# Gate and up as seven products of quadrant sums, and eight tile buffers for the first norm of a two-layer hybrid decoder kernel

## The reference

```python
    mix = jnp.concatenate([hm, ha, hs], axis=-1) @ w_out
    x = x + rms_norm(mix, norm_w[1])
    h = rms_norm(x, norm_w[2])
    ff = (jax.nn.silu(h @ w_gate) * (h @ w_up)) @ w_down
    return x + rms_norm(ff, norm_w[3])
```

## Time and profile before

| | us |
|---|---|
| median of 3 runs | 2903.09 |
| lowest and highest of the 3 | 2901.5 and 7317.59 |
| profiled execution, its own time | 2905.06 |
| profiled execution, span of the trace | 2903.3 |

### The profile page before, as it was taken

How to read it: one execution, slowest core, us unless ns; L and a number is a source line. 1 busy time by engine, 2 the same in 40 slices (tenths; PEclk the granted TensorE clock), 3 DMA queues, 4 the chain that set the end, 5 groups by cost and what they waited for, 6 DMA issues and landing times. The chain is left out here.

```text
span 2903.3 us, 34251 instructions
## 1 busy us (share of the span) xinstructions
PE 2810.1 (97%) x13396; PEld 2261.9 (78%) x13396; DVE 1229.7 (42%) x2170; ACT 924.5 (32%) x1618; POOL 906.3 (31%) x450
## 2 busy tenths in 40 slices
PE   6999999999999999999989999998999999999997
PEld 5677877778888888888766788777788888888886
DVE  4479854574111122211355799547640122211115
ACT  4336433563211111111243374346632111111112
POOL 1238410330332333222343383104303232222234
PEclk9999999899999999999999999999999999999999
DMA  4102310522211111111321133106221111111113
GB/s 131 44 23 87 116 57 19 151 88 95 74 44 51 58 43 58 43 43 43 116 80 30 30 95 111 59 15 179 81 89 50 58 44 57 43 43 43 51 45 137
DMA packets 232832, 197.72 MB, mean 68 GB/s; under 512 B 20352, under 2 KB 208896, under 8 KB 232592
## 3 DMA queue, kind: packets, MB, share of 16 engines
q1 hardware_dynamic: 226960, 175.26, 20.0%
q10 hardware_dynamic: 5760, 20.97, 1.9%
HBM read 157.41 MB, written 38.80 MB: 68 GB/s over the span
## 5 line engine op out<-in xcount | busy, mean ns | idle before, releaser
L2125 PE MATMUL ps<-act_hi,whi 128*128 128x512 f32 x1408 | 548.4, 389 | 0.0
L2125 PE MATMUL ps<-act_hi,wlo 128*128 128x512 f32 x1408 | 548.1, 389 | 0.0
L2125 PE MATMUL ps<-act_lo,whi 128*128 128x512 f32 x1408 | 547.7, 389 | 0.0
L2189 DVE TENSOR_TENSOR hf<-sg,ps 128x1024 f32<-128x1024 f32 x44 | 53.7, 1221 | 891.4 <-PE ps L2125 891.4
L834 PE MATMUL ps<-act_hi,whi 128*128 128x512 f32 x960 | 395.2, 412 | 15.5 <-ACT smr L383 10.6
L834 PE MATMUL ps<-act_hi,wlo 128*128 128x512 f32 x960 | 378.9, 395 | 0.0
L834 PE MATMUL ps<-act_lo,whi 128*128 128x512 f32 x960 | 378.6, 394 | 0.0
L2002 POOL TENSOR_TENSOR wlo<-raw,whi 128x1024 fp32r<-128x1024 f32 x88 | 210.0, 2395 | 489.3 <-ACT whi L2048 489.3
L1247 DVE TENSOR_SCALAR_CACHE_REDUCE ties<-score,kth 128x384 uint8<-128x384 f32 (+5 forms) x396 | 348.4, 943 | 5.1 <-issue 0.4
L2196 DVE TENSOR_TENSOR yacc<-yacc,ps 128x1024 f32<-128x1024 f32 x176 | 214.8, 1220 | 248.5 <-PE ps L2157 248.5
L2125 PEld LDWEIGHTS ps<-act_lo,whi 128*128 128x128 f32 x1408 | 264.3, 188 | 55.2
(11 more groups left out here) (304 smaller groups left out, 3974.6 us busy)
## 6 DMA issues: line engine op xcount, KB each, us to landing
raw<-in_w_in SPq DMA_DIRECT2D x56, 512.0 KB, 3.9
raw<-in_w_up SPq DMA_DIRECT2D x44, 512.0 KB, 4.0
raw<-in_w_gate SPq DMA_DIRECT2D x44, 512.0 KB, 3.8
raw<-in_w_down SPq DMA_DIRECT2D x44, 512.0 KB, 3.6
proj_scratch<-stage ACTq DMA_DIRECT2D x40, 512.0 KB, 2.7
wc<-proj_scratch SPq DMA_DIRECT2D x14, 1280.0 KB, 6.7
xmid_scratch<-xres SPq DMA_DIRECT2D x16, 512.0 KB, 2.6
resid<-xmid_scratch SPq DMA_DIRECT2D x14, 512.0 KB, 5.5
```

What stands on the lines that cost most here:

```text
L2125: mm = pe.matmul(ps[:, 2 * s + half, :], w[:, k], a[:, k, cols], start=(k == 0 and m == 0), stop=(k == KT - 1 and m == 2))
L2189: v.tensor_tensor(hf[:, :], sg[:, :], unit_psum(1), ALU.mult).then_inc(hidden.sem, 1)
```

## The change

**Seven products.** For a block of 256 columns the product (256 columns × 1024 inputs) × (1024 inputs × 1024 tokens) is seen as 2×2 quadrants: input halves of 512, column units of 128, token halves of 512. Instead of eight quadrant products it computes seven products of sums of quadrants, and forms the four result quadrants by adding and subtracting them. A product is 4 k-slices × 3 = 12 matmuls of the same shape as before; gate and up of a block are 14 products. The down part keeps its 96 matmuls per block.

- The seven token forms (`form_hi`, `form_lo`, 128×2048 each) are built once per layer at the end of D, by ACT, DVE and POOL: ACT now copies the transposed tile to `normed_q` in float32 (`untransposed`), DVE adds quadrants (`token_sum`), ACT rounds (`token_hi`), DVE or POOL subtracts (`token_lo`). Parts that need only tiles 0 to 6 (EARLIER, 3/4) are done apart from those of tile 7 (LAST, 1/4).
- The weight forms are built for every block: 10 sums on DVE (`form_sum_part`, 128×512), 14 copies on ACT (`form_hi_part`), 14 subtractions on POOL (`form_lo_part`), in a ring of six slots shared with the down weights. Slot reuse waits for the product five places earlier.
- Results are gathered in SBUF (`gate_t`, `up_t`): per seven products ACT does 2 copies out of PSUM (`first_product`) and DVE 10 adds or copies of 128×512 (`drain`). Silu and the multiplication then work from SBUF in four pieces of 128×512.
- The order on PE is: gate of block 0; then for each k up(k), gate(k+1), down(k); at the end up(10) and down(10) with nothing between. `hhi`/`hlo` have one buffer now. Weight loads are 1 MB each.
- POOL clears `yacc` only after the last token form, since the buffers overlap.

**Eight tile buffers.** In layer 0 the tiles 4 to 7 of x go to the not yet used `score` buffer, and all eight loads stand ahead of the small weights.

**Placement.** All of SBUF is laid out anew by address. The constants `cst` are loaded again in layer 1, the small weights of layer 1 are loaded at the end of E instead of the start, and the residual and norm row loads for the end of E wait for products of up(10).

```diff
-                    sp.dma_start(tap[t % 4][:, :], x_in[t * P:(t + 1) * P, :]).then_inc(xa_in[t % 4].sem, 16)
+                    sp.dma_start(x_place(t), x_in[t * P:(t + 1) * P, :]).then_inc(xa_in[t].sem, 16)
...
+        WEIGHT_SUM = {1: ((0, 1), (1, 1), ALU.subtract), 2: ((0, 0), (1, 1), ALU.add), 3: ((1, 0), (0, 0), ALU.subtract),
+                      4: ((1, 0), (1, 1), ALU.add), 6: ((0, 0), (0, 1), ALU.add)}
+        PRODUCT_BANK = (0, 1, 2, 3, 0, 1, 2)
+        DRAINED = {1: 2, 2: 4, 3: 6, 4: 7, 5: 9, 6: 10}
...
+                def product(i, f, slot, r):
+                    pe.wait_ge(*f_lo(L, f + 1))
+                    later = not (isinstance(r, int) and r == 0)
+                    if i == 0 and later:
+                        pe.wait_ge(*m_drain(L, 10 * (r - 1) + DRAINED[4]))
...
+                    if i == 4:
+                        pe.wait_ge(*m_first(L, r + 1))
+                    if i == 5:
+                        pe.wait_ge(*m_drain(L, 10 * r + DRAINED[1]))
...
+                    wh, wl = flat_form(ring_hi[slot]), flat_form(ring_lo[slot])
+                    for k in range(4):
+                        for m, (w, a) in enumerate(((wh, form_hi[i]), (wh, form_lo[i]), (wl, form_hi[i]))):
+                            mm = pe.matmul(ps[:, PRODUCT_BANK[i], :], w[:, k], a[:, k], start=(k == 0 and m == 0), stop=(k == 3 and m == 2))
+                    mm.then_inc(f_done.sem, 1)
...
+                pe.wait_ge(*t_lo_p(L, 2))
                 pe.wait_ge(*d_mix(L, NT - 1))
-                half_unit(0, 0)
+                product(0, 0, 5, 0)
+                product(1, 1, 0, 0)
                 turn_normed(pe, NT - 1)
...
+                for i in range(2, 7):
+                    pe.wait_ge(*t_lo_v(L, i + 1))
+                    if i == 3:
+                        pe.wait_ge(*t_lo_p(L, 3))
+                    product(i, i, (i + 5) % 6, 0)
...
+                for i in range(7):
+                    product(i, f0 + i, i % 6, up_item(k))
+                pe.wait_ge(*m_drain(L, 10 * (2 * FB - 1) + DRAINED[5]))
+                down(k, f0 + 7, (1, 2, 3, 4), last_bank, N < DEPTH)
...
+                def form_sum_part(i, f, slot, place):
+                    v.wait_ge(*f_in[place[0]](L, 16 * place[1]))
+                    v.wait_ge(*f_done(L, f - 5))
+                    a, b, op = WEIGHT_SUM[i]
+                    v.tensor_tensor(flat_form(ring_sum[slot]), weight_part(ff_raw[place[0]], *a), weight_part(ff_raw[place[0]], *b), op)\
+                     .then_inc(f_sum.sem, 1)
...
+                pool.wait_ge(*t_lo_v(L, 7))
+                pool.wait_ge(*t_lo_p(L, 3))
+                for t in range(NT):
+                    ins = pool.memset(yacc[t][:, :], 0.0)
...
+                for j in range(6):
+                    form_lo_part(j, 7 + j, j, (1, 1))
```

More of the change, by code:

```diff
@@ L141, in build @@
         ps = ctx.enter_context(nc.psum_tensor("ps", [P, 8, HALF], F32))
[L144 to L154, removed]
+        ident = sb("ident", [P, P])
         small = sb("small", [P, 96])
@@ L169, in build @@
[L169 to L193, removed]
-        ties = ab("ties", [P, sum(width[2:])], U8)
@@ new lines, in build @@
+        mrow = after("mrow", [P, S])
+        arow = after("arow", [P, S])
+        gcol = after("gcol", [P, NT, 4, MH])
+        scol = after("scol", [P, NT, 4, SH])
+        scol_minus = after("scol_minus", [P, NT, SH])
+        iwc = after("iwc", [P, NT, AH])
+        decm = after("decm", [P, 2, NT])
+        decs = after("decs", [P, SH, NT])
+        convc = after("convc", [P, KT, 8])
+        assert top[0] == CHUNKS
+        tap = [after(f"tap{k}", [P, S]) for k in range(4)]
+        score = after("score", [P, sum(width)])
@@ new lines, in build @@
+        avr = after("avr", [P, NT, AH * HD])
+        aq = after("aq", [P, 2, S])
+        ak = after("ak", [P, 2, S])
+        iq = after("iq", [P, 2, S])
+        stage = [after(f"stage{s}", [P, 3 + S]) for s in range(2)]
+        ik = after("ik", [P, S])
+        smr = after("smr", [P, S])
+        ties = after("ties", [P, sum(width[2:])], U8)
+        kth = after("kth", [P, NT - 2])
+        held = after("held", [P, NT - 2])
+        TAIL = CHUNKS + 101536
+        DOWN0 = TAIL - 4 * KB
+        assert top[0] <= TAIL - 12 * KB
@@ new lines, in gate, with hid_hi @@
+                def gate(k, n):
+                    act.wait_ge(*m_drain(L, 20 * k + (1, 7, 8, 10)[n]))
+                    act.activation(piece(gate_t, n), piece(gate_t, n), ACT.Silu).then_inc(silu.sem, 1)
+                def hid_hi(k, n):
+                    act.wait_ge(*hidden(L, 4 * k + n + 1))
+                    if n == 0 and not (isinstance(k, int) and k == 0):
+                        act.wait_ge(*y_ps(L, NT * k))
+                    act.activation(piece(hhi, n), piece(up_t, n), ACT.Copy).then_inc(h_hi.sem, 1)
@@ L2139, in turn_next, with down @@
+                def down(k, f, slots, place, turning=False):
                     def turn_next(t):
```

899 lines of the change are left out of this document (578 added, 321 removed).

## The result

The changed kernel takes 2872.12 us (median of 4, 2872.01 to 2876.19) against 2905.56 for before (median of 4, 2901.5 to 7317.59). The ratio is 0.9895, 95% interval 0.9883 to 0.9907: 1.0% less, some 31 us. One execution of before, the 7317.59, lies far off the others and is not in this ratio. The time lies within the range; the forecast of 2841 promised 62 us, twice the gain.

A forecast was written before the change was run, and what follows sets the result against it. PE was taken as the bound, in stage E by the number of matmuls alone. 2903.3 − 119.6 + 48.0 + 11.3 − 2.0 = 2841.0 us for the span, forecast 2841; range 2823 to 2876, the forecast's own 2832 to 2850.

The forecast's parts named there:

- So in stage E only the number of matmuls counts: Gate, up and down stage: 528 fewer matmuls at 0.2265 us save 119.6 us, if other engines stay ahead.
- the steady part: Repeating blocks of E: DVE, POOL and ACT work fits beside PE's 59.8 us a block, so 0 cost.
- five products' lead: Loop of E: a weight form is due five products, 13.6 us, after its slot is free.
- rival 3: Down to up in E: the ring's lead is too short, 1.5 us per block in 20 blocks, 2871; chance 0.15.
- rival 4: Down to up in E: longer chain plus slow clock, 3.7 us in each of 20 blocks, 2915; chance 0.05.
- From D into E: Turn once per layer: building the forms leaves PE waiting, costing 24.0 us a layer, 48 us in two.
- the forecast's walk: Engine queues followed from the last w_out tile at 730.6 to the end of up(0) at 795.7 us.
- rival 1: Turn from D into E: DVE and POOL waits mostly miss each other, 2 × 6.5 us less, 2828; chance 0.15.
- rival 2: Turn from D into E: POOL wins the race before tile 7's statistics, 2 × 6 us more, 2853; chance 0.10.
- The end of E: Once per layer, down(10) waits 3.9 us, then slow clock 1.7: 5.6 us, 11.3 in two layers.
- The start: Start of layer 0: eight buffers bring tile 4 in time, 2 us off, bounds 0 and 4.3.

The follow-up runs named there:

- experiment 3: Two runs: the changed kernel with pads so E's operands lie at the same address modulo 512 bytes, 2842.44 us; before with 32 bytes ahead of dhi and dlo, 2915.11 us.
- aligned: The changed kernel with pads so that forms, ring buffers, hidden buffers and w_out's parts lie at the same address modulo 512 bytes; 2842.44 us, ratio to before 0.9784.
- best2: The changed kernel with pads, later yacc memsets, split down wait, and form 3's first three quarters subtracted on DVE, behind product 2's needs; 2821.05 us.
- best3: best2 with ACT's two copies of product 0 out of PSUM moved ahead of its parts of token forms 5 and 6; 2818.24 us, ratio to before 0.9713.
- the three small kernels: Kernels computing nothing of the reference: groups of 96 back-to-back matmuls at stage addresses, shifted moving operands, or two address pairs in turn; 226.7 to 237.7 ns at 512 columns.
- m1_pitch: First small kernel, computing nothing of the reference: groups of 96 back-to-back matmuls with each stage's operand addresses; before's 0.2267 us each, the changed kernel's product 0 0.2333.
- g16: Group of 96 matmuls in m1_pitch with the first group's addresses beside DMA loads; 21.80 us.
- g11: Group of 96 matmuls in m1_pitch with before's addresses beside ScalarE alone; 21.76 us.

## Why the prediction was wrong, and where it was right

**The step that failed** is "So in stage E only the number of matmuls counts": the unit price of a number of matmuls by a pitch. The 528 removed matmuls were rightly priced, 119.6 us. But the forecast took for granted that the remaining ones keep 0.2265 us, and gave the steady part 0. They cost 0.2329 and 0.2314, 1.49 us a block, 33 us by the loop's pitch, as the change moved every operand of E to new addresses and at 512 columns the pitch depends on these. Put back to matching addresses with nothing else changed, the stage gave back 14.8 and 14.6 us (experiment 3), together the 29.4 that the sum was short by. My cover, five products' lead, was an argument about waits, and no wait came. The time of 2872 is where rival 3 stood (2871), but by another mechanism: there is no idle TensorE in the loop, so rivals 3 and 4 did not happen.

The trace of before held a hint that I passed over. Its mixing products have the same shape as those of E, and next to no idle time, but other durations, 399 to 406 ns where E has 389. One of its three groups by line:

```profile
L1635 PE MATMUL ps<-wohi,act_lo 128*128 128x512 f32 x256 | 102.4, 400 | 0.0
```

In before wohi lies at 32 modulo 256 for six of the eight k and at 192 for two, act at 128. In aligned, where they agree, this group is at 395, and a mixing stage is 2.05 us shorter than in after. That it is not at 389 there stays open.

**From D into E: right.** From the end of the last mixing tile (726.73 in after, 730.6 in the forecast's walk) to the norm of tile 7: 12.0 us, said 11.6; to product 2: 21.3, said 21.2; to the end of `first_product`: 31.9, said 32.5; to product 5: 36.5, said 36.4; to up(0): 44.5, said 44.7; slow clock in up(0) 1.6, said 1.3. The mutual exclusion of DVE and POOL, read from two rows of before, carried it. So rival 1 falls. Of rival 2 the first half came: POOL won the race. DVE's three ring sums were open for 6.30 us, and ScalarE, with their copy ahead in its queue, began tile 7's statistics 1.90 us behind the end of the mixing (728.63), where before began them at once (730.62 and 730.59). But of the 6 us of this rival next to nothing arrived: the norm of tile 7 was done 0.4 us later than in the walk.

**The end of E: right.** Idle 4.15 and 3.96 us, said 3.9; the slow clock 1.7 in layer 1, said 1.7. Removing the wait gave back 4.9 and 5.8 us, said 5.6.

**The start: right in kind.** 2.65 us for the buffers at the first projection product, said 2.0, within 0 and 4.3, though only 0.74 of it was seen at the end of the mixing; ACT's copy of the small weights came at 18.55, said 19.3.

The whole balance: from the last mixing product of a layer to the next stage A or the end, before 742.0 and 738.3 us, after 726.1 and 723.3, so 16.0 and 15.0 less. The forecast's terms are −59.8 + 24.0 + 5.65. With half of the 33 us for the pitch, +16.4, they give −13.8; with what aligned shows that the addresses cost in this stretch, +14.8 and +14.6, they give −15.4 and −15.6. The difference between 16.4 and these is likely the turn, where the products wait anyway: up(0) starts 44.9 us behind the mixing in aligned and 44.5 in after, no earlier for the shorter pitch. Some 0.6 us a layer, of either sign, are not assigned.

## What to carry to other kernels

Price an instruction that stays as carefully as one that goes: when a change moves buffers, the same matmul can cost 3% more, and no wait, no idle time and no clock shows it, only the distance between starts and, by 10 ns, the mean duration. For products of 512 columns in fp32r, put stationary and moving operands at the same place modulo 256 bytes, on a multiple of 32 (common shifts of 32 and 64 bytes were fast, one of 4 slow); here 900 bytes of pads were worth as much as the whole change. And where TensorE waits for several engines in a row, find the one whose work is longest before reordering: best2 and best3 moved the gap twice and never closed it.

## What the runs showed of the hardware that was not expected

- The pitch of a 128x128 by 128x512 fp32r product back to back is 226.7 ns when all stationary and moving operands lie at the same place modulo 256 bytes, and 228.9 to 237.7 ns in the other cases that were run, one of them with both operands 4 bytes on. After a change of place the first 3 to 9 products of a fast group are still slow, by the starts in the traces of the three small kernels. The Trainium skill (TensorE: Matmul & The Clock Gate, section Step-by-step: what each phase is for) says that the streaming and the stationary operand have an SBUF read port each. By that alone their relative place should cost nothing, and here it costs up to 10 ns a product, so the measurement decides. For 256 columns it does not hold (120.0 aligned, 117.7 with 32 bytes between).
- VectorE, ScalarE and GpSimd at work beside it do not change the pitch: the windows of m1_pitch show 21.79 us for 96 products beside VectorE, where the first seven settle as said, and 21.76 beside all three. Beside DMA loads (g16, DMA share 0.28) it is 21.80, with nine products that settle.

```profile
274.94:296.73 21.79, 21.79 (x98) 18.02 (x96) 14.15 (x24) 3.91 (x8) 0.00 (x0) 1.00 0.01 1
...
340.25:362.01 21.76, 21.76 (x98) 18.02 (x96) 21.76 (x14) 18.87 (x37) 21.76 (x14) 1.00 0.00 0
```

- The same windows show what VectorE and GpSimd do to each other: 14 operations each in 21.76 us, 1.55 us apiece for VectorE, where VectorE without GpSimd did 24 in 14.15 us (0.59). ScalarE keeps its pace, 37 operations in 18.87 us, 0.51 apiece, against 29 in 14.96 in the window 296.73 to 318.49 of g11. The Trainium skill (GPSIMD Engine Reference, section 1) says that GpSimd's SBUF interfaces are shared with VectorE; the trace agrees with it again.
